# GpSimd's order in the attention stage of a hybrid decoder step: v issued before and behind the inversion, the second multiplication last

## The reference

```python
for w, d in ((128, 1), (512, 4), (2048, 16)):       # three patterns
    # every query reads keys at distances 0, d, 2d, ... w (129 of them)
    s = q @ k.T * scale + bias                      # band of 128 + 128 keys
    lse = logsumexp(s); o = exp(s - lse) @ v
o = sum over patterns of softmax(lse)[pattern] * o[pattern]
a = o * silu(g)
```

## Time and profile before

| | us |
|---|---|
| median of 3 runs | 3117.1 (3112.88 to 3119.91) |
| the profiled execution | 3116.27 |
| its span (first to last instruction) | 3114.6 |
| TensorE busy | 2679.1 (86%) |
| VectorE, ScalarE, GpSimd busy | 1231.6, 884.5, 875.7 |
| first and last phase's mark L1107 (phases 0 and 14) | 1452.14, 2153.87 |
| granted TensorE clock, mean | 0.932 |

### The profile page before, as it was taken

The page is one execution under the profiler, slowest core; times in us unless marked ns, Lnnn a source line. Parts: engine busy times, 40 slices in busy tenths (PEclk is TensorE's granted clock), DMA queues, the critical chain, the costliest instruction groups (busy, mean ns, idle before and its releaser), DMA issues. The chain is left out here.

```text
span 3114.6 us, 43720 instructions
## 1 busy us (share of the span) xinstructions
PE 2679.1 (86%) x16598; PEld 2369.3 (76%) x16598; DVE 1231.6 (40%) x3327; ACT 884.5 (28%) x1935; POOL 875.7 (28%) x679
## 2 busy tenths in 40 slices
PE   7899999999999999968898889889359999405699
PEld 7799999999978888847898889888247777302585
DVE  3245445200000154415565556555155555373321
ACT  3212222222111111113454445446154444100100
POOL 1054545222121131210323332334323333141000
PEclk9999999999999999988999999999679999757899
DMA  4224354421231111145455655563446565383542
GB/s 156 85 69 109 106 150 136 128 70 59 72 128 68 54 64 59 41 123 131 113 124 124 146 128 126 122 150 87 116 135 190 182 200 166 121 306 129 211 145 79
DMA packets 197764, 381.87 MB, mean 123 GB/s; under 512 B 62659, under 2 KB 119979, under 8 KB 184476
## 3 DMA queue, kind: packets, MB, share of 16 engines
q1 hardware_dynamic: 158748, 242.40, 24.8%
q0 software_dynamic: 36160, 132.25, 16.7%
q10 hardware_dynamic: 2672, 4.74, 0.5%
HBM read 259.71 MB, written 124.96 MB: 124 GB/s over the span
## 5 line engine op out<-in xcount | busy, mean ns | idle before, releaser
L118 PE MATMUL bank<-w_hi,hT_hi 128*128 128x256 f32 x1792 | 508.2, 284 | 14.0 <-DMA ident<-ident 11.6
L120 PE MATMUL bank<-w_hi,hT_lo 128*128 128x256 f32 x1792 | 504.9, 282 | 0.0
L119 PE MATMUL bank<-w_lo,hT_hi 128*128 128x256 f32 x1792 | 503.4, 281 | 0.0
L1141 PE MATMUL obank<-turned_p,v_in 128*128 128x128 f32 (+1 forms) x1632 | 324.6, 332 | 74.6 <-issue 68.2
L1098 PE MATMUL front<-k_hi,q_st 128*128 128x256 f32 x768 | 323.3, 429 | 38.7 <-DMA k_lo<-qk 28.6
L118 PEld LDWEIGHTS bank<-w_hi,hT_hi 128*128 128x128 f32 x1792 | 339.0, 189 | 14.9 <-DMA ident<-ident 11.9
L120 PEld LDWEIGHTS bank<-w_hi,hT_lo 128*128 128x128 f32 x1792 | 339.3, 189 | 0.0
L119 PEld LDWEIGHTS bank<-w_lo,hT_hi 128*128 128x128 f32 x1792 | 338.9, 189 | 0.0
L1141 PEld LDWEIGHTS obank<-turned_p,v_in 128*128 128x128 f32 x1632 | 255.3, 197 | 92.4 <-issue 69.4
L1261 ACT ACTIVATE score<-score,ntop_sb 128x256 f32<-128x256 f32 (+1 forms) x768 | 290.2, 455 | 4.9 <-DMA ntop_t<-ntop 4.5
L1099 PE MATMUL front<-k_lo,q_st 128*128 128x256 f32 x768 | 276.4, 368 | 0.0
(11 more groups left out here) (282 smaller groups left out, 4826.1 us busy)
## 6 DMA issues: line engine op xcount, KB each, us to landing
qk<-xc_in SPq DMA_DIRECT2D x64, 512.0 KB, 5.0
w_raw<-w_in POOLq DMA_DIRECT2D x26, 1024.0 KB
q_st<-qk POOLq DMA_DIRECT2D x32, 512.0 KB
k_hi<-qk POOLq DMA_DIRECT2D x32, 512.0 KB
k_lo<-qk POOLq DMA_DIRECT2D x32, 512.0 KB
v_in<-v_out POOLq DMA_DIRECT2D x16, 1024.0 KB, 8.8
cum_all<-cum SPq DMA_DIRECT2D x16, 1024.0 KB, 10.0
xcT<-xc SPq DMA_DIRECT2D x12, 1024.0 KB
```

Of the source, the lines that this page charges most:

```text
L118: pe.matmul(out, lhs_hi(k), rhs_hi(k), start=k == 0, stop=False)
L119: pe.matmul(out, lhs_hi(k), rhs_lo(k), start=False, stop=False)
L120: last = pe.matmul(out, lhs_lo(k), rhs_hi(k), start=False, stop=k == KT - 1)
L1141: last = pe.matmul(obank[m["bank"]][:, m["col"]:m["col"] + m["n"]], v_in[:, p, (P + 1) * m["v"][1] + P * b:(P + 1) * m["v"][1] + P * b + P ...
```

## The change

GpSimd's program is put in another order in the odd phases, and the function that normalised is cut in two. v of the widest pattern is issued right behind q and k; then comes the inversion; then v of the middle pattern; and the second multiplication comes last. The waits that each load had (`mixed` at 4 lots and 12 lots) stay with it. Even phases keep their order: in them only the name of the function changes.

```diff
-            def normalise(h, b):
+            def invert(h):
                 pool.wait_ge(den_moved, 64 * h + 32)
                 pool.tensor_tensor(den_in[:, :], den_in[:, :], minus_one[:, :], ALU.pow).then_inc(recip_done, 1)
+
+            def normalise(h, b):
                 pool.wait_ge(den_moved, 64 * h + 64)
                 pool.tensor_tensor(acc[o_rows(b), b, :], acc[o_rows(b), b, :], recip[o_rows(b), :], ALU.mult).then_inc(finished, 1)
                 pool.wait_ge(finished, h + 1)
@@
                     load_qk(h + 3)
+                if h % 2 == 1 and h + 1 < H:
+                    pool.wait_ge(mixed, NG * h + 4)
+                    load_v(pool, 2, (h + 1) // 2)
+                if h >= 1:
+                    invert(h - 1)
+                if h % 2 == 1 and h + 1 < H:
+                    pool.wait_ge(mixed, NG * h + 12)
+                    load_v(pool, 1, (h + 1) // 2)
                 if h >= 1:
                     normalise(h - 1, (h - 1) % 2)
-                if h % 2 == 1 and h + 1 < H:
-                    for p, lots in ((2, 4), (1, 12)):
-                        pool.wait_ge(mixed, NG * h + lots)
-                        load_v(pool, p, (h + 1) // 2)
             apply_gate(H - 1, 1, H // 2 - 1)
+            invert(H - 1)
             normalise(H - 1, 1)
```

## The result

| | before | after |
|---|---|---|
| median of 15 runs each, us | 3118.45 (3110.30 to 3125.75) | 3087.28 (3075.44 to 3111.38) |
| ratio to before, 95% interval | | 0.9908 (0.989 to 0.9927) |
| measured again later (4 runs beside 7 of before) | 3117.33 | 3081.14; ratio 0.9876 (0.986 to 0.9893) |
| profiled execution / span | 3116.27 / 3114.6 | 3075.44 / 3073.8 |

What follows compares the result with a forecast made beforehand. TensorE bounds the kernel, idling for late v at even phases' starts. Replacing 13.8 us a pair by 5.4 of store wait plus 2.4 of clock gains 36 us in six pairs: 3081 us, range 3068 to 3093.

Steps and rivals of the forecast that it cites:

- The wait for v goes: Start of even phases 2 to 12: TensorE's wait for v and its slow clock vanish, 13.8 us a pair, 82.6 in all.
- What is late next: Even phases: store of head h - 2 delays ScalarE's odd-lot copy; 1.4 us of new wait even if nothing moves.
- landed at T + 39.7: Odd phases, T the mark of phase 3: the inverse's 8 KB write lands 39.7 us later, held by the widest pattern's v.
- Wrong if the small write lands as early as before: Sign in the changed profile that the inverse's write is not held by v, pointing to the rival forecast of 3060.
- rival A: Odd phases: v does not hold the inverse's small write; 9.5 us gained a pair, 57 in all, 3060; chance 0.22.
- the tail of v or nothing: Odd phases: the read of recip meets little or no v traffic; 0.7 us of it in some pairs.
- 4.0: Delay in us of the store through the inverse's round trip in odd phases; bounds 0 to 9.8.
- The wait of 5.4 us: Even phases: TensorE waits 5.4 us before its product with lot 3, behind the late store and odd-lot copy.
- The clock: Even phases: the new TensorE wait drops the clock to 0.50 again, charged 2.4 us a pair.
- The sum: Per pair of phases: 5.4 + 2.4 = 7.8 us in place of 13.8; 6.0 gained, 36 in six.

Runs made afterwards that it cites:

- e2: Changed kernel with the load of v of the widest pattern put last, behind the second multiplication, in odd phases: 3126.72 us in one run (before 3118.42).
- e5: Changed kernel without the second multiplication, acc stored without it, all loads and the read of recip kept: 3020.11 us in one run (before 3118.99).
- e1: Changed kernel with the load of v of the middle pattern back behind the second multiplication: 3058.31 us, ratio 0.9811 to the kernel before.
- e3: Changed kernel with v of the widest pattern issued ahead of q and k in odd phases: 3077.4 us, ratio 0.9867 to the kernel before.
- e4: Changed kernel with the inversion put ahead of q and k in all phases: 3058.59 us, ratio 0.9804 to the kernel before.
- e10: Changed kernel with the inverse's round trip ahead of q and k, also earlier on SyncE, and the middle pattern's v last: 3029.41 us, ratio 0.9714 to before.
- e6: Changed kernel with widest v, then six 512 KB loads in 512 B pieces, before the inversion; q and k behind it in all phases: 3125.57 us, one run.

## Why the prediction was right

The time came out, and so did the next waiter, the store; of the chain in front of the store one step was wrong, and a second error of the other sign hid it. Point by point:

- The wait for v goes, 6 x 13.8 us (82.8, where the text has 82.6): right. None is left in the changed kernel, and e2, which puts V16 back, brings it back. e5 confirms the 44.25 us of a phase without waits, thirteen times, on which 13.8 rests.
- What is late next is the store, by way of L1282 (now L1289) and the odd lot behind it: right, and shown by e5. The landing takes 1646.15 - 1641.66 = 4.5 us and the copies 1.9, as taken.
- The step that failed: the write of the inverse "landed at T + 39.7", held by the widest pattern's v. Measured in phase 3: T + 36.8, against 36.1 before, and 10.4 to 11.9 us from the write to the read in the six odd phases, where 15 had been said. By the prediction's own sign ("Wrong if the small write lands as early as before") this step was wrong. The 8 KB write is not held by v beyond q and k (the statement of rival A), but the read of recip, to which I gave "the tail of v or nothing", takes 4.85 us more. The two errors stand against each other in the sum, and that is luck: the multiplication moved by 5.5 us in phase 3 and about 5 over the six, not 4.0. With the write right and the read as it was taken, the sum would have been that of rival A, 3060. e1 and e3 show the read's share of each load in phase 3: 4.6 with neither, 5.9 with V16, 7.05 with V4, 9.45 with both; over the six odd phases 4.4 to 5.3, 4.9 to 5.9, 5.4 to 7.9 and 8.7 to 9.9.
- The wait of 5.4 us is 5.73 in the mean of six, and comes at 12.5 us in phase 4 where 11.5 was said.
- The clock: 96.55 - 88.5 - 5.73 leaves 2.3 us a pair, where 2.4 was charged. Not all of that is the clock. The even phases are 1.3 to 2.3 us longer than 44.25 and their wait, 1.8 in the mean; the other 0.5 lies in the odd phases, at a granted clock of 1.00. The 2.4 had been taken from a whole pair too. The clock ran slow in the first third of the even phase, as said.
- The sum: 96.5 us a pair forecast, 96.55 measured; 36 us, against 34.6 by the marks in one profiled execution and 29 and 39 us by the two ratios.

What the prediction did not ask is what each half of the change is worth. e1 gives it: V4, issued 2.5 us behind the mark of the even phase, was not waited for. It needed no earlier place, and in that place it takes the read from 5.9 to 9.45 us.

Left open: why the write passes V16 but waits for q and k. It took 1.4 to 1.5 us in most phases with nothing in front (e4, e10), landed at about the end of everything issued before it in e6 and in the kernel before, yet ahead of the end of V16 in e1 (shown above) and in the changed kernel. The size of the pieces does not explain it (e6). Nor does a wait for all that was issued before: the write is 128 packets of 64 B in the traces. In phases 1 to 12 of the kernels before and after, with V16 behind q and k and without it, the first of them ran 6.1 to 6.3 us after the issue and half of them had run after 8.0 to 8.6 us, while the DMA engines were full until 9.9 us after the issue in phase 3 of the kernel before. The loads had by then moved 1.7 MB since the issue of the write, in e6 1.6 MB. That looks like a stock of bulk of a fixed size already taken on when a small DMA comes, and not like a place in one common line; it would also give the read's late start and e4's slow store. It is an inference from these traces, and no run varied that size. In e6 and in the kernel before only 2.0 MB were left to move, so there the two accounts can hardly be told apart.

## What to carry to other kernels

When a wait is taken away, work out the slack of the next waiter first; here the store that frees a buffer would have been late by 1.4 us behind a wait of 11, and every microsecond added in front of it then counted. Put a small round trip through DRAM on its way before bulk loads are issued, and issue each bulk load as late as its own reader allows: the same six loads of v cost a pair of phases nothing (e10) or 13.8 us (before), by the order of GpSimd's and SyncE's queues alone. Of a change that moves two loads, measure each alone.

## What the runs showed of the hardware that was not expected

- An 8 KB write takes 1.4 us alone and 10.4 to 12.5 us behind 3 MB of q and k issued some 6 to 8 us before it (kernels before and after); issued in the same microsecond as the first of them it takes 1.4 (e4). Another 1 MB issued between them and it does not make it later.
- The loads of v, and those of e6 in pieces of 512 B, move at 283 to 297 GB/s, q and k, in rows of 8 KB, at 195 to 213. The size of the pieces alone does not give that: the read of recip, also in rows of 8 KB, moved at 262.
- TensorE's waits of 4.4 to 6.5 us dropped the granted clock to 0.50, in phase 4 from 1644.0 to 1654.2, and made the even phases 1.3 to 2.3 us longer beyond the waits themselves. In e1 waits of 2.7 to 3.4 us dropped it too, one of 1.7 us did not.
